# Stage seams of a two-layer decoder step: moved loads, a shorter overflow loop, and unread products on TensorE

## The chip, the cores and the metric

The kernel runs on one core of one Trainium2 chip. The metric is the device time of one execution in microseconds (us), as the median of several runs.

## What is computed

One inference step of a two-layer hybrid decoder: 1,024 prompt tokens and 8 sample tokens of width 1,024, all in 32-bit floats. In each layer an input projection feeds three head groups, a short gated convolution, a latent attention with 8 heads, and an mLSTM with 4 heads. Their outputs are normalised per head and projected back. A hierarchical mixture of 32 experts (two per token) and a gated embedding term follow.

```python
z = jnp.einsum('bld,dn->bln', x, w_in)
q = jnp.einsum('blr,rn->bln', rms_norm(c_q, q_norm_g), w_uq).reshape(B, L, MLA_HEADS, QK_NOPE + QK_ROPE)
h1 = layer_norm(DN_ALPHA * x + jnp.einsum('blm,md->bld', y, w_out), ln1_g, ln1_b)
moe = hier_moe(h1.reshape(B * L, D), w_group, b_group, w_expert, b_expert, e_gate, e_up, e_down).reshape(B, L, D)
ple = jnp.einsum('blp,pd->bld', p, w_pe) * jax.nn.sigmoid(jnp.einsum('bld,de->ble', h1, w_pg))
out = layer_norm(DN_ALPHA * h1 + moe + ple, ln2_g, ln2_b)
```

## The kernel before, in words

The tokens stand in nine tiles of 128 rows: eight of the prompt, and a ninth (`LAST`, also `TP`) with the 8 samples. Each engine has its own program, written out by hand, and the programs meet only in semaphores. A layer has four stages, and each ends in a `Phase`, whose exit is a barrier of all engines, one round for each unbroken range of semaphores that it clears (line 114).

- **Projection** (`stream_project_prepare`). TensorE (PE) walks over the tiles. In step `t` it projects tile `t` in pieces (`part`, lines 507 and 519), and between the pieces it does the small products of tile `u = t - 1`: latents turned (536 to 538), gates turned (545), queries (556), keys (563), values (568), gate columns (573), mLSTM scores (579), queries turned (590). The queue of SyncE (SP) has its own order: in step `t` it stores what tile `u` made, with the store of its turned queries (`QT`) at line 433 and that of the mLSTM output at line 438. In a tenth step (`t == NT`) it loads the first head pair for attention (`first.load_qk`, `first.load_v`, lines 218 to 227), and after that stores the samples' latents (408, 409) and turned queries (433). SP then waits for all its stores (line 449) before it joins the barrier. In layer 1 the stage starts by adding gathered expert rows (DVE line 693, semaphore `added`) to the residual and normalising; PE waits for the result before its first transposes (line 492).
- **Attention** (`attention`) begins with the scores of line 1149, followed by mask, maximum and exponential on DVE and ACT, then transposes (1159).
- **Sample attention** (`sample_attention`) first turns weights (1631 to 1633), waits for copies on DVE, multiplies them with the queries (1636), turns cached pages (1585, 1592), and ends with the product of line 1668.
- **Output, routing and experts** (`mix_route_experts`) begins with products of lines 2259, 2122 and 2148. Later it goes through `EARLY = (0, 1, 2, 3, TP, 4)`: a gate product per tile on PE (2220; 2130 for the samples), its sigmoid on ACT (2474, 2487), a turned embedding input (PE 2187, copied by ACT at 2459, function `p_copied`), and a result stored by ACT to `BASE` (`stored_base`, line 2470, two buffers, semaphore `base_stored`). At the same time the rows are scattered to the experts by GpSimd. Then 21 groups of expert rows run, each stored by ACT at line 2505. Rows over an expert's capacity would go through `rest_turns`, which is in the program of SP, PE, ACT and DVE: two rounds of a loop with sixteen copies of its body each, every copy under an `If`. No line of these bodies shows in the trace.

`combine_last` ends the program: for each tile PE sums the base rows (line 2956) and two gathered expert rows with their weights (2960) in one of four accumulators, then comes a layer norm on DVE and ACT, and a store. SP loads all nine base tiles at once, with gain and bias after the first (2927, 2930), and GpSimd issues all eighteen gathers in a row (2945). PE starts when ACT has made all 18 diagonal weight tiles (`diag_ready`, line 3007).

## Time and profile before

| what | value |
|---|---|
| median of 3 runs | 2455.68 us (2449.44 to 2460.41) |
| the profiled execution, its own time | 2454.07 us |
| its span in the trace | 2452.3 us |
| mean granted TensorE clock | 0.965 |
| busy share of the span: PE, DVE, ACT, POOL | 92%, 47%, 30%, 14% |
| HBM traffic | 208 GB/s over the span |

All rows come from one profiled execution. Times count from the start of its span. A product of 32-bit floats shows as two records on PE, and "x8" counts records. The granted clock is a share of full speed: 1.00 is 2.4 GHz, 0.50 is 1.2 GHz, and a value between them is a stretch with both.

### The profile page before, as it was taken

Reading aid. Unit: us, or ns where it says so; the run is one execution under the profiler, and the core shown is the slowest. Engines: PE = TensorE matmul, PEld = TensorE weight load, DVE = VectorE, ACT = ScalarE, POOL = GpSimd, SP = SyncE. Lnnn points to the kernel's source line nnn. Section 1 sums busy time; section 2 is a strip of 40 time slices with the busy share of each in tenths; the row PEclk is TensorE's granted clock in tenths of the full one; section 3 lists DMA queues with packets and bytes.
Section 4 is the critical chain, followed back from the end, with each engine's and each line's share of the span. In section 5 each row is a group of like instructions: output and inputs, shape, how many; then the busy total and the mean of one; then the engine's idle time right before and its main releaser. Section 6 shows DMA issues by size and latency. Waiting matters only on the chain. (4 is left out here: it accounts for less than half of the span.)

```text
span 2452.3 us, 39565 instructions
## 1 busy us (share of the span) xinstructions
PE 2246.9 (92%) x14448; PEld 1164.2 (47%) x14448; DVE 1160.3 (47%) x2954; ACT 729.4 (30%) x1454; POOL 335.6 (14%) x514
## 2 busy tenths in 40 slices
PE   7999987989999999999599999688889999999977
PEld 3555554557455443333255555455655544333323
DVE  3444444665686312322345554466568752222226
ACT  2555553543211011000145545444323011110012
POOL 1021006830000200000100000296000020000011
PEclk9999998998999999999799999899899999999998
DMA  9476127733510869999753421565323146899976
GB/s 342 161 261 237 59 60 191 198 71 122 193 56 5 347 238 363 406 420 420 260 186 94 129 69 51 151 191 146 122 73 147 31 188 256 343 374 421 420 299 248
DMA packets 229654, 512.00 MB, mean 209 GB/s; under 512 B 60614, under 2 KB 138382, under 8 KB 204088
## 3 DMA queue, kind: packets, MB, share of 16 engines
q1 hardware_dynamic: 182760, 385.68, 43.6%
q0 software_dynamic: 27136, 85.62, 9.8%
q10 hardware_dynamic: 19552, 38.02, 4.2%
q8 instruction: 121, 1.98, 0.3%
q14 instruction: 85, 0.70, 0.1%
HBM read 382.90 MB, written 126.32 MB: 208 GB/s over the span
## 5 line engine op out<-in xcount | busy, mean ns | idle before, releaser
L507 PE MATMUL pj_zp<-pj_w,pj_xT 128*128 128x512 f32 (+1 forms) x1280 | 504.5, 541 | 5.9 <-DMA pj_w<-in_w_in 5.9
L507 PEld LDWEIGHTS pj_zp<-pj_w,pj_xT 128*128 128x128 f32 x1280 | 225.5, 192 | 204.4 <-issue 193.0
L2325 PE MATMUL op_bank<-ex_wgu,h 128*32 128x512 f32 x2688 | 297.1, 594 | 3.2 <-DMA ex_wgu<-in_e_up 3.2
L2148 PE MATMUL op_bank<-op_wout,op_hT 128*128 128x512 f32 x512 | 226.9, 601 | 3.1 <-DVE h L2632 1.7
L2869 DVE TENSOR_TENSOR ex_h<-ex_sil,op_bank 128x256 f32<-128x256 f32 x42 | 17.7, 421 | 367.1 <-ACT ex_sil L2513 367.1
L2325 PEld LDWEIGHTS op_bank<-ex_wgu,h 128*32 128x32 f32 x2688 | 84.5, 110 | 190.6 <-issue 187.4
L2345 PE MATMUL op_bank<-ex_wd,ex_hT 128*32 128x512 f32 x1344 | 154.6, 601 | 8.9 <-DMA ex_wd<-in_e_down 7.4
L2148 PEld LDWEIGHTS op_bank<-op_wout,op_hT 128*128 128x128 f32 x512 | 97.4, 193 | 120.7 <-issue 118.4
L1248 ACT ACTIVATE at_p<-at_s,at_nmx 128x640 f32<-128x640 f32 (+7 forms) x128 | 94.8, 740 | 172.7 <-DVE at_nmx L1211 172.1
L2513 ACT ACTIVATE ex_sil<-op_bank 128x256 f32<-128x256 f32 x42 | 16.1, 383 | 423.7 <-PE op_bank L2325 423.7
L1159 PE MATMUL at_tp<-ident,at_p 128*128 128x128 f32 x576 | 88.3, 281 | 35.8 <-DVE at_pT L1217 25.2
L2220 PE MATMUL op_bank<-op_wpg,op_hT 128*128 128x512 f32 x256 | 115.6, 606 | 0.0
L2111 POOL DMA_INDIRECT scratch_XR<-h,route_row x36 | 36.6, 1018 | 523.8 <-DVEq L2839 513.4
L1209 DVE TENSOR_REDUCE at_mx<-at_s 128x1 f32<-128x640 f32 (+7 forms) x128 | 97.0, 758 | 4.5
L1149 PE MATMUL at_s<-first_qk 96*128 96x512 f32 (+3 forms) x192 | 78.2, 523 | 21.1 <-PEq L114 21.1
L950 ACT ACTIVATE pj_z<-pj_zp 128x512 f32<-128x512 f32 (+1 forms) x80 | 43.2, 540 | 176.3 <-PE pj_zp L507 176.3
L1159 PEld LDWEIGHTS at_tp<-ident,at_p 128*128 128x128 f32 x576 | 62.5, 141 | 65.8 <-issue 60.5
L478 POOL DMA_INDIRECT pj_r<-scratch_YR,route_row x18 | 18.9, 1052 | 540.9 <-issue 357.5
L1207 DVE TENSOR_TENSOR at_s<-at_s,at_mask 128x128 f32<-128x128 f32 x128 | 38.3, 300 | 103.0 <-PE at_s L1149 101.1
L2246 PE MATMUL op_bank<-op_wpg,op_hT 128*128 128x512 f32 x192 | 84.4, 593 | 0.0
L2345 PEld LDWEIGHTS op_bank<-ex_wd,ex_hT 128*32 128x32 f32 x1344 | 40.9, 110 | 91.0 <-issue 84.8
L2220 PEld LDWEIGHTS op_bank<-op_wpg,op_hT 128*128 128x128 f32 x256 | 49.4, 196 | 59.9 <-issue 59.7
(486 smaller groups left out, 3453.2 us busy)
## 6 DMA issues: line engine op xcount, KB each, us to landing
ex_wgu<-in_e_gate SPq DMA_DIRECT2D x64, 1024.0 KB, 11.6
ex_wgu<-in_e_up SPq DMA_DIRECT2D x64, 1024.0 KB, 15.0
ex_wd<-in_e_down SPq DMA_DIRECT2D x64, 1024.0 KB, 18.0
h<-scratch_XR SPq DMA_DIRECT2D x42, 512.0 KB, 16.9
scratch_XR<-pj_zero POOLq DMA_DIRECT2D x38, 512.0 KB, 7.8
pj_w<-in_w_in SPq DMA_DIRECT2D x8, 2048.0 KB, 17.9
pc_ckv<-in_cache_ckv SPq DMA_DIRECT2D x200, 64.0 KB, 2.0
cv_cch<-scratch_Z POOLq DMA_DIRECT2D x48, 256.0 KB, 4.3
```

Of the source, the lines that this page charges most:

```text
L507: last = pe.matmul(zp[c % ZB][:, 0:cn], xT[:, t % 2, k, :], w[:, k, c0:c0 + cn], start=(k == 0), stop=(k == KC - 1), skip_group_check=True)
L950: act.activation(z[:, t % 2, c0:c0 + cn], zp[c % ZB][:, 0:cn], ACT.Copy).then_inc(z_ready, 1)
L1149: last = pe.matmul(scores_of(n)[:, c:min(c + 512, width)], queries(j, s)[:, qb * P:(qb + 1) * P], keys(j, s)[:, c:min(c + 512, width)], st ...
L1159: last = pe.transpose(tp[e][:, kb % 4, :], probs[small(n)][units[n][1]][:, kb, :], ident[:, :])
L1207: st.did(dve.tensor_tensor(diag, diag, mask[:, :], ALU.add))
L1209: st.did(dve.tensor_reduce(mx[:, k:k + 1], out[:, 0:(qb + 1) * P], AX.X, ALU.max))
L1248: act.activation(probs[small(n)][s][:, 0:qb + 1, :].rearrange("p b n -> p (b n)"), scores_of(n)[:, 0:(qb + 1) * P], ACT.Exp, bias=nmx[:, k ...
L2148: last = pe.matmul(op[n][:, :], hT[:, t, c, :], wout[:, c, n * 512:(n + 1) * 512], start=(c == 0), stop=(c == KC - 1))
L2220: last = pe.matmul(gpair[i % 2][n][:, :], hT[:, t, c, :], wpg[:, c, n * 512:(n + 1) * 512], start=(c == 0), stop=(c == KC - 1))
L2246: last = pe.matmul(dbank[:, :], hT[:, DEFERRED[j], c, :], wpg[:, c, n * 512:(n + 1) * 512], start=(c == 0), stop=(c == KC - 1))
L2325: last = pe.matmul(gu[q % 2][part], xT[q % 2][:, c, part], wgu[s][:, :, c, :], start=(c == 0), stop=(c == KC - 1), skip_group_check=True)
L2345: last = pe.matmul(yp[n][part, :], heT[:, q % 2, c, part], wd[s][:, c, n * 512:(n + 1) * 512], start=(c == 0), stop=(c == 1), skip_group_c ...
```

## The change

It has five parts.

1. In the projection stage SP now stores the samples' latents and loads the first head pair inside step `LAST`, ahead of the mLSTM output's store; the tenth step is gone, and the samples' turned queries are stored by ACT at the end of its program (semaphore `q_last`).
2. In the `EARLY` loop, ACT's turn for the samples copies two embedding inputs and issues the base store of the tile before, and only then waits for the older base store and computes the sigmoid.
3. `rest_turns` is one loop over one copy of its body, and the whole loop stands under `If(used > 0)`.
4. In `combine_last`, base loads and gathers run at most two tiles ahead, gain and bias are loaded with tile 2, PE waits for the diagonals of one tile at a time, and the base products run two tiles ahead.
5. `kept_busy` issues products of the identity (128 columns) with the identity repeated four times (512 columns), into a bank that nobody reads. They stand at nine places: four in layer 1 before the first transposes; in both layers 2, 1, 1 and 5 in the projection's tail, 2 after attention, 2 and 3 in sample attention; 2 in `combine_last`.

```diff
@@ -227,6 +227,11 @@
+def kept_busy(pe, bank, ident, count):
+    for _ in range(count):
+        pe.matmul(bank, ident[:, :], ident[:, :].unsqueeze(1).broadcast_to([P, 4, P]), start=True, stop=True)
+
+
 def stream_project_prepare(nc, d, layer, ident, cache, first):
@@ -355,6 +361,24 @@
                     sp.dma_start(w[:, :, c0:c0 + cn], of_layer(d["w_in"], layer).rearrange("(p k) n -> p k n", k=KC)[:, :, c0:c0 + cn]).then_inc(w_loaded[n], 16)
+
+                def latents_stored(u, n):
+                    sp.wait_ge(lat_ready, u + 1)
+                    sp.dma_start(of_layer(d["ckv_all"], layer)[rows(u, n)], ckvn[0:n, :]).then_inc(c_stored, 16)
+                    sp.dma_start(of_layer(d["krope_all"], layer)[rows(u, n)], kpad[0:n, NOPE:]).then_inc(c_stored, 16)
+
+                def first_pair_loaded():
+                    sp.wait_ge(k_stored, 16 * TP)
+                    sp.wait_ge(q_stored, 16 * TP)
+                    sp.wait_ge(normed, NT)
+                    first.load_qk(sp, d, 0)
+                    sp.wait_ge(turned, 2 * NT)
+                    for s in range(2):
+                        sp.wait_ge(y_kept[s], 16 * len(range(s, NT, 2)))
+                    first.load_qk(sp, d, 1)
+                    sp.wait_ge(v_stored, 16 * TP)
+                    sp.wait_ge(o_ready, NT)
+                    first.load_v(sp, d)
@@ -386,27 +410,12 @@
                 sp.wait_ge(cache.table_loaded, 16)
-                for t in range(NT + 1):
+                for t in range(NT):
                     u = t - 1
...
                         load(t + 3)
-                    if t == NT:
-                        sp.wait_ge(k_stored, 16 * TP)
-                        sp.wait_ge(q_stored, 16 * TP)
-                        sp.wait_ge(normed, NT)
-                        first.load_qk(sp, d, 0)
-                        sp.wait_ge(turned, 2 * NT)
-                        for s in range(2):
-                            sp.wait_ge(y_kept[s], 16 * len(range(s, NT, 2)))
-                        first.load_qk(sp, d, 1)
-                        sp.wait_ge(v_stored, 16 * TP)
-                        sp.wait_ge(o_ready, NT)
-                        first.load_v(sp, d)
-                    if is_tile(u):
-                        n = P if u < LAST else DECB
-                        sp.wait_ge(lat_ready, u + 1)
-                        sp.dma_start(of_layer(d["ckv_all"], layer)[rows(u, n)], ckvn[0:n, :]).then_inc(c_stored, 16)
-                        sp.dma_start(of_layer(d["krope_all"], layer)[rows(u, n)], kpad[0:n, NOPE:]).then_inc(c_stored, 16)
+                    if is_chunk(u):
+                        latents_stored(u, P)
                     if t < TP:
@@ -427,12 +436,14 @@
                         sp.dma_start(d["V"][rows(u)], v[:, :]).then_inc(v_stored, 16)
-                    if is_tile(u):
-                        n = P if u < LAST else DECB
+                    if is_chunk(u):
                         sp.wait_ge(qT_out, 2 * u + 2)
-                        sp.dma_start(d["QT"][:, :, rows(u, n)].rearrange("h p n -> p h n"), qT[:, :, 0:n]).then_inc(q_stored, 16)
+                        sp.dma_start(d["QT"][:, :, rows(u)].rearrange("h p n -> p h n"), qT[:, :, :]).then_inc(q_stored, 16)
                     if t + 2 < NT:
                         keep(t + 2)
+                    if t == LAST:
+                        latents_stored(LAST, DECB)
+                        first_pair_loaded()
                     if is_chunk(u):
@@ -442,7 +453,8 @@
                 sp.wait_ge(v_stored, 16 * TP)
-                sp.wait_ge(q_stored, 16 * NT)
+                sp.wait_ge(q_stored, 16 * TP)
+                sp.wait_ge(q_last, 16)
                 sp.wait_ge(y_stored, 16 * TP)
@@ -632,6 +644,9 @@
+                if not entry:
+                    pe.wait_ge(added, 1)
+                    kept_busy(pe, f[0][:, :], ident, 4)
                 rows_turned(0)
@@ -646,6 +661,9 @@
                     part(t, 2)
+                    if t == LAST:
+                        pe.wait_ge(xT_ready, 2 * NT)
+                        kept_busy(pe, f[4][:, :], ident, 2)
                     if is_chunk(u):
@@ -658,6 +676,9 @@
                         values(u)
+                        if t == LAST:
+                            pe.wait_ge(q_out, 2 * u + 2)
+                            kept_busy(pe, f[4][:, :], ident, 1)
                         gate_columns(u)
@@ -668,8 +689,12 @@
                         state_turned()
+                    if t == LAST:
+                        kept_busy(pe, f[4][:, :], ident, 1)
                     if is_tile(u):
                         queries_turned(u)
+                    if u == LAST:
+                        kept_busy(pe, zp[1][:, :], ident, 5)
                     part(t, 8)
@@ -1047,6 +1072,8 @@
                     projected_out(t, 4)
+                act.wait_ge(qT_out, 2 * NT)
+                act.dma_start(d["QT"][:, :, rows(LAST, DECB)].rearrange("h p n -> p h n"), qT[:, :, 0:DECB]).then_inc(q_last, 16)
@@ -1193,6 +1220,7 @@
                         output_turned(n - 2)
+                kept_busy(pe, sc[2][:, :], ident, 2)
@@ -1631,6 +1659,7 @@
                 pe.transpose(misc[0:ROPE, DECB:2 * DECB], krn[:, :], ident[0:DECB, 0:DECB]).then_inc(prep, 1)
+                kept_busy(pe, scp[0][:, :], ident, 2)
                 pe.wait_ge(q_ready, 1)
@@ -1667,6 +1696,7 @@
                 last.then_inc(att_done, 1)
+                kept_busy(pe, scp[0][:, :], ident, 3)
@@ -1855,11 +1884,10 @@
-    with eng.Fori(0, -(-BLOCKS // REST_STEP)) as r:
-        with eng.If(REST_STEP * r < used):
-            for i in range(REST_STEP):
-                with eng.If(REST_STEP * r + i < used):
-                    yield REST_STEP * r + i
+    with eng.If(used > 0):
+        with eng.Fori(0, BLOCKS) as b:
+            with eng.If(b < used):
+                yield b
@@ -2474,17 +2502,20 @@
                 for i, t in enumerate(EARLY):
+                    if t == TP:
+                        p_copied(P_ORDER.index((i, 0)))
+                        p_copied(P_ORDER.index((i - 3, 1)))
+                        stored_base(i - 1)
+                        act.wait_ge(base_stored[i % 2], 16 * (i // 2))
+                        act.wait_ge(g_done, 2 * i + 2)
+                        act.activation(sig[:, i % 2, 0:SCOLS], gpair[i % 2][0][:, 0:SCOLS], ACT.Sigmoid).then_inc(sig_done, 2)
+                        continue
                     if i >= 2:
                         act.wait_ge(base_stored[i % 2], 16 * (i // 2))
-                    if t < TP:
-                        sigmoid(i, 0)
+                    sigmoid(i, 0)
                     if i >= 2:
                         p_copied(P_ORDER.index((i, 0)))
-                    if t < TP:
-                        sigmoid(i, 1)
-                    else:
-                        act.wait_ge(g_done, 2 * i + 2)
-                        act.activation(sig[:, i % 2, 0:SCOLS], gpair[i % 2][0][:, 0:SCOLS], ACT.Sigmoid).then_inc(sig_done, 2)
+                    sigmoid(i, 1)
                     if i >= 3:
@@ -2924,10 +2955,12 @@
                 for t in range(NT):
-                    sp.dma_start(base[:, t, :], d["BASE"][rows(t)]).then_inc(loaded[t], 16)
-                    if t == 0:
+                    if t >= 2:
+                        sp.wait_ge(gathered[t - 2], 32)
+                    if t == 2:
                         for buf, which in ((g, "ln2_g"), (b, "ln2_b")):
                             sp.dma_start(buf[:, :], row_of_layer(d[which], layer)).then_inc(gains, 16)
+                    sp.dma_start(base[:, t, :], d["BASE"][rows(t)]).then_inc(loaded[t], 16)
                 for t in range(NT):
@@ -2939,6 +2972,8 @@
                     m = P if t < TP else DECB
+                    if t >= 2:
+                        pool.wait_ge(gathered[t - 2], 32)
                     if t == TP:
@@ -2947,19 +2982,29 @@
             def _(pe):
-                pe.wait_ge(diag_ready, 2 * NT)
-                for t in range(NT):
+                def bases(t):
                     pe.wait_ge(loaded[t], 16)
...
                         pe.matmul(acc[t % 4][:, n * 512:(n + 1) * 512], ident[:, :], base[:, t, n * 512:(n + 1) * 512], start=True, stop=False)
+
+                def gathered_rows(t):
+                    pe.wait_ge(diag_ready, 2 * t + 2)
                     pe.wait_ge(gathered[t], 32)
...
                         last.then_inc(summed, 1)
+
+                kept_busy(pe, acc[0][:, 0:512], ident, 2)
+                bases(0)
+                bases(1)
+                for t in range(NT):
+                    gathered_rows(t)
+                    if t + 2 < NT:
+                        bases(t + 2)
```

## Rows read from the trace of the kernel before

**Rows 1.** The page's line of the granted TensorE clock, 40 equal slices.
```profile
PEclk9999998998999999999799999899899999999998
```
**Rows 2.** Stages: stretch, length, then busy us (records) of PE, PEld, DVE, ACT, POOL; PEclk, DMA, GB/s.
```profile
340.00:345.00 5.00, 4.97 (x40) 2.29 (x44) 3.65 (x9) 1.53 (x4) 0.00 (x0) 0.68 0.00 1
...
370.00:375.00 5.00, 0.00 (x0) 0.00 (x0) 0.00 (x0) 0.00 (x0) 0.00 (x0) 0.55 1.04 228
...
380.00:385.00 5.00, 5.00 (x14) 2.48 (x13) 2.72 (x7) 1.66 (x4) 3.34 (x9) 0.58 0.95 247
```
**Rows 3.** Timeline of PE, projection's end, layer 0: start, us, instruction, idle before and its releaser.
```profile
339.56 0.38 PE L545 MATMUL pj_f<-ident,ml_gz 128*4 128x128 f32 x2 [1.92 <-DVE ml_gz L769]
...
360.31 0.38 PE L536 MATMUL pj_f<-ident,mp_cqn 128*128 128x128 f32 x2
...
378.69 5.98 PE L1149 MATMUL at_s<-first_qk 96*128 96x512 f32 x10 [10.33 <-PEq L114]
```
**Rows 4.** Timeline of SP's queue over the same stretch.
```profile
358.39 0.32 SPq L433 DMA_DIRECT2D scratch_QT<-mp_qT  x1
...
365.71 0.33 SPq L218 DMA_DIRECT2D first_qk<-scratch_QT  x1
...
367.88 0.39 SPq L227 DMA_DIRECT2D first_v<-scratch_V  x1
```
**Rows 5.** DMA issues from 335 to 382 us: count, KB each, median us to landing.
```profile
first_v<-scratch_V SPq DMA_DIRECT2D x1, 512.0 KB, 8.8
...
scratch_KT<-mp_kT SPq DMA_DIRECT2D x1, 384.0 KB, 3.2
```
**Rows 6.** Timeline, start of sample attention, layer 0.
```profile
556.39 3.58 PE L1636 MATMUL sa_misc<-sa_qT,sa_wukT 64*128 64x8 f32 x16 [1.57 <-DVEq L1720]
...
559.90 3.67 PE L1585 MATMUL sa_tp<-ident,pc_ckv 128*128 128x128 f32 x16
...
564.93 2.02 PE L1585 MATMUL sa_tp<-ident,pc_ckv 128*128 128x128 f32 x16
```
**Rows 7.** Timeline, end of sample attention and start of the output stage, layer 0.
```profile
611.36 1.06 PE L1668 MATMUL sa_misc<-sa_wuv,sa_ol 128*8 128x64 f32 x16 [0.32 <-DVE sa_ol L1755]
...
615.32 0.99 PE L2259 MATMUL op_bank<-ms_g,ms_rep 32*128 32x197 f32 x2 [2.90 <-PEq L114]
...
618.95 9.18 PE L2148 MATMUL op_bank<-op_wout,op_hT 128*128 128x512 f32 x16 [0.73 <-DVE op_hT L2614]
```
**Rows 8.** Timeline, samples' turn of the `EARLY` loop, layer 0.
```profile
828.09 7.03 PE L2220 MATMUL op_bank<-op_wpg,op_hT 128*128 128x512 f32 x16
...
844.93 0.38 ACT L2459 ACTIVATE op_pT<-op_bank 128x256 f32<-128x256 f32 x1 [8.78 <-DMA scratch_BASE<-op_sig]
...
845.46 0.67 PE L2187 MATMUL op_bank<-ident,op_p 128*128 128x128 f32 x2 [2.85 <-ACT op_pT L2459]
...
847.93 9.05 PE L2220 MATMUL op_bank<-op_wpg,op_hT 128*128 128x512 f32 x16
```
**Rows 9.** Timeline of ACT, last issue of layer 0's experts.
```profile
1179.93 0.34 ACTq L2505 DMA_DIRECT2D scratch_YR<-op_hT  x1
```
**Rows 10.** Line 114, the barrier, 1178 to 1187 us: ns min/median/max, first to last start.
```profile
L114 ACTq DRAIN x5: 8/8/8, 1183.5 to 1185.7; - x5
```
**Rows 11.** Timeline of PE, start of layer 1.
```profile
1208.40 14.00 PE L507 MATMUL pj_zp<-pj_w,pj_xT 128*128 128x512 f32 x26 [3.51 <-DMA pj_w<-in_w_in]
```
**Rows 12.** Timeline, `combine_last`.
```profile
2392.04 6.67 PE L2960 MATMUL fi_acc<-fi_r,fi_diag 128*128 128x512 f32 x8 [3.79 <-DMA fi_r<-scratch_YR,route_row]
...
2398.55 1.88 PE L2956 MATMUL fi_acc<-fi_base,ident 128*128 128x512 f32 x4
...
2400.26 3.60 PE L2960 MATMUL fi_acc<-fi_r,fi_diag 128*128 128x512 f32 x8
```
**Rows 13.** The chain of waits: start, us, what.
```profile
2381.51 10.48 DMA fi_r<-scratch_YR,route_row
```
**Rows 14.** DMA issues, 1165 to 1222 us.
```profile
pj_r<-scratch_YR,route_row POOLq DMA_INDIRECT x6, 7.6
```

More of the change, by code:

```diff
@@ L325, in stream_project_prepare @@
             ph.sem(n) for n in ("q_done", "q_out", "k_done", "k_out", "v_done", "v_out", "r_steps", "rope_out", "qt_done", "qT_out"))
-        c_stored, k_stored, v_stored, q_stored, y_stored = (ph.sem(n) for n in ("c_stored", "k_stored", "v_stored", "q_stored", "y_stored"))
+        c_stored, k_stored, v_stored, q_stored, y_stored, q_last = (
+            ph.sem(n) for n in ("c_stored", "k_stored", "v_stored", "q_stored", "y_stored", "q_last"))
         qk_done, qk_out, g_steps, g_neg, g_exp, g_sum, g_ln, gate_ready, gate_done, gate_out = (
@@ L1823 @@
 LEAD = 2
-REST_STEP = 16
 P_ORDER = ((0, 0), (1, 0), (2, 0), (3, 0), (0, 1), (4, 0), (1, 1), (5, 0), (2, 1))
```

## The prediction

> **What bounds the kernel now.** I read the line of the granted clock first [rows 1]: nearly every slice of about 61 us stands at nine tenths of full speed or more, and the dips, eights and sevens, come few and far between. With PE busy for 92% of the span, PE is the bound, and what can be won without less work is its idle time and the time at half clock. The stretches of 5 us show where that is [rows 2]: at the end of the projection PE works at 0.68, then it stands idle while the DMA engines are full (1.04), and it begins attention at 0.58. Rows 3 show the wait itself: 10.33 us ahead of line 1149. SP's queue and the landings [rows 4, 5] say what it waits for: the last load is issued at 367.88 and lands 8.8 us later, at 376.7; the barrier follows. Similar holes stand before sample attention, before the output stage and in the samples' turn [rows 6 to 8], after the experts [rows 9, 10], at the start of layer 1 [rows 11], and ahead of the last sums [rows 12, 13]. Where I saw the stage in layer 0, I count layer 1 as its copy.
>
> **The price of an unread product.** Eight records with 512 columns take 3.60 us at full clock and 6.67 at half [rows 12]; a product is two records, so 0.9 or 1.67 us. The change adds 16 products in layer 0, 20 in layer 1 and 2 at the end: 38, which is 34 us at full and 63 at half clock. They are free only where a wait covers them.
>
> **The change part by part**, as gains:
>
> Projection's tail, the first four products. The two ahead of line 545 fall into its wait of 1.92 us [rows 3]. If they hold the clock, the 4.97 us of busy time at 0.68 [rows 2] shrink by a third, 1.6. I count that once; the two single products and whatever else the tail gains end in front of the loads, which set the stage's end. Bounds 0 and 1.6.
>
> SP's order. The store of the last full tile's turned queries is issued at 358.39 [rows 4], and its twin for the keys lands in 3.2 [rows 5], so it is done at 361.6; the normed latents are ready too, since PE turns them at 360.31 [rows 3]. The loads, now issued at 365.71, can go 4.1 earlier, and so does their end: 376.7 becomes 372.6, attention starts at 374.6, and two layers give **8.2**. Moved behind the loads are the last mLSTM output's store on SP, which finds about 2 MB ahead of it in the DMA engines (some 9 us of loads at 228 GB/s [rows 2]), and the samples' turned queries, which leave by ACT's queue. Both must land before the barrier, which is why I take bounds of 2 and 6 a layer, from half of the gain to half more. SP now waits earlier for the key, query and value stores; queued behind that wait are only those loads and that one store.
>
> Five products in that wait. They take 4.5 us at full and 8.4 at half clock, and the wait that is left is 10.33 − 4.1 = 6.2: they fit if the clock is up. Line 1149 takes 5.98 us at 0.58 [rows 2, 3] and would save about 3. The DMA tail may leave PE idle again after them, so I take 0.8 a layer, **1.6**; bounds 0 and 3 a layer.
>
> Sample attention. The same product group of line 1585 takes 3.67 us early and 2.02 later [rows 6], 1.65 lost to the clock; line 1636 would give half of 3.58, 1.8, and what runs between them about 0.7: up to 4.1 a layer. Two products behind attention may hold back the barrier by 1.8. I take 3 a layer, **6**; bounds −1.8 and 4.1.
>
> Output stage. Line 2148 takes 9.18 us for 16 records where line 2220 takes 7.03 for the same shape [rows 7, 8]: 2.1. Line 2259 gives 0.5 and the products between them about 1.0 by estimate, 3.6 in all. Against that, line 1668 ends at 612.42, and three products last until 615.1, while the stage starts at 615.32 after its barrier [rows 7]. The barrier cannot end before PE joins it, and its rounds are (1185.7 − 1183.5) / 4 = 0.55 us apart [rows 10]; I price the delay at two rounds, 1.1, and take 1.8 a layer after a little more is lost, **3.6**; bounds −2.7 and 3.6.
>
> Samples' turn. ACT stands 8.78 us in front of line 2459, waiting for the base store two tiles back; PE waits 2.85 for that copy and then takes 9.05 for line 2220 in place of 7.03 [rows 8]. With the copies ahead of the wait both go: 2.85 + 2.02 = 4.9, **10** for two layers; bounds 2.85 (the clock stays as it is) and 6. Behind ACT's remaining wait stands only the samples' sigmoid, 8 rows whose result is wanted a tile later.
>
> The overflow loop. ACT issues its last store at 1179.93, done at 1180.27, and the first drain comes at 1183.5 [rows 9, 10]: 3.2 us in which nothing shows but the branches. One test in place of two rounds of tests should leave about 1.2, a gain of 2 a layer, **4**; bounds 0 (a last landing holds the barrier) and 6.4 in all. The Trainium skill (Runtime: NRT & Kernel Launch, Instruction fetch mechanics) says that a branch to a place that isn't fetched yet stalls for a DMA fetch; jumps over large bodies would then be the whole 3.2, and the sum would take 6.4 here. No row above shows such a fetch.
>
> Start of layer 1. PE waits 3.51 us for the weights ahead of line 507 [rows 11], so a faster clock before it gains nothing, and 507 itself can save 14.00 − 26 × 0.45 = 2.3. The four products, 6.7 us at half clock, could overrun that cover by 3.2. I take **0** between −3.2 and 2.3.
>
> `combine_last`. A gather lands after 10.48 us beside the other loads [rows 13], while those at the start of layer 1 take 7.6 [rows 14]: 2.9. The first group of line 2960 loses 6.67 − 3.60 = 3.1 to the clock, and tile 1's base product, some 1.88 with its second half [rows 12], moves ahead into the wait, 1.7: at most 7.7. But base 2 is now loaded only after the first gathers landed, behind gain and bias, and PE comes to it right after the first group; I price that new wait, with the dip that follows it, at 3.7, half of the 7.7. The output store on SP stands behind the base loads and has slack. **4**; bounds 0 and 7.7.
>
> The sum is 1.6 + 8.2 + 1.6 + 6 + 3.6 + 10 + 4 + 0 + 4 = 39. The profiled execution took 2454.07 (its span 2452.3), which gives 2415; the median of the runs is 1.6 higher, so the forecast is **2417**.
>
> **The rivals.** *The products don't hold the clock, only the reorderings count.* For: the waits are cut into pieces by semaphores, and PE at the end of the projection was busy and still at 0.68 [rows 2]. Against: the later groups of a stage show how soon continuous work brings it back [rows 6]. Gain: 8.2 + 2 × 2.85 + 4 = 17.9, time 2438.
> *All of it works.* 1.6 + 8.2 + 6 + 8.2 + 5 + 10 + 6.4 + 6 = 51.4, time 2404; the overflow loop counts here with its full 3.2 a layer. The stall is then in the branches themselves and goes with them. The Trainium skill's section named above states this rule.
> *The samples' turn gives nothing*, because the experts behind it wait for the scatter or for DMA: 39 − 10 = 29, time 2427.
> *Slower: the products stand in the way.* Where a wait is shorter than its products at half clock (1.92 against 3.3 ahead of line 545, 2.90 against 5.0 ahead of the output stage [rows 3, 7]), the engine that waits for PE comes late. If that held for all 38, they would cost 63, the reorderings would give 17.9, and the time would be 2501. It decides from the point at which the products outlast the waits by more than 17.9 + 12 in sum. Against: the waits of 10.33 and of 3.79 [rows 3, 12] are longer than that.
>
> **How the numbers follow.** The forecast gets 0.45, with a range of its own of 2405 to 2429; reorderings alone 0.22; all of it 0.20; no gain in the samples' turn 0.08; slower 0.05. A measurement of this kernel can tell about 0.5%, some 12 us, from no change, so faster means under 2443. The low end, 2402, leaves out the lower half of the case where all works; the high end, 2440, takes in most of the reorderings alone and leaves out the slower case. Faster 0.87, the same 0.08 (the upper end of the reorderings alone), slower 0.05.
>
> **What would show it.** Right: SP's first load of the head pair issued near 361.6 and attention starting near 374.6; a full clock in the first 5 us of attention, sample attention and the output stage; no wait on the base store ahead of line 2459's copy in the samples' turn, and 7.03 for the group after it; a drain about 1 us after ACT's last issue; line 2960's first group at 3.60 and about 3 us earlier. Wrong: PE idle still at the seams with the clock at half behind it; the base store or the mLSTM output's store as the last landing before a barrier; new waits of PE on base tiles in `combine_last`; or unread products as the last instructions of PE ahead of a barrier at which all the others already wait.

## The result and the profile after

The changed kernel takes 2420.0 us (median of 4 runs, 2419.1 to 2420.1), the kernel before 2457.6 beside it: a ratio of 0.9851, with a 95% interval of 0.9832 to 0.9869. The forecast was 2417, the range 2402 to 2440. The profiled execution after has a span of 2418.3 us, 34.0 less than the profiled one before.

On the page, PE's busy share and its clock rose. The chain that ended last has changed hands: before it was mostly PE's last sums,

```profile
PE 2%; DMA 0%; DVE 0%; issue 0%; ACT 0%; POOL 0%; POOLq 0%
```

and now it is DMA and DVE:

```profile
PE 2262.0 (94%) x14524; PEld 1160.5 (48%) x14524; DVE 1159.9 (48%) x2954; ACT 730.4 (30%) x1454; POOL 337.6 (14%) x514
...
PEclk9999999999999999999899999999999999999998
...
DMA 2%; DVE 1%; issue 0%; POOL 0%; ACT 0%; POOLq 0%; SPq 0%; ACTq 0%
```

The dips of [rows 1] are all but gone. PE is busy for 15 us more (2246.9 before; the products), and the program still ends 34 us earlier.

To see where, I cut PE's timeline of each profile at the same instructions: the first product with the input weights, the first of attention, of sample attention, of the output stage, the first and the last of the experts. Lengths in us, layer 0 / layer 1; the columns "again" are second profiles of the same two kernels, and the last two are runs told of below.

| stage | before | before, again | after | after, again | reordering only | products only |
|---|---|---|---|---|---|---|
| projection to attention's start | 361.5 / 361.3 | 359.0 / 362.8 | 355.7 / 359.0 | 355.9 / 358.8 | 358.3 / 359.0 | 357.7 / 359.0 |
| attention | 174.0 / 174.1 | 174.1 / 174.2 | 175.4 / 173.3 | 175.0 / 171.5 | 176.4 / 174.3 | 176.2 / 173.4 |
| sample attention | 62.6 / 63.5 | 62.7 / 63.6 | 59.5 / 60.3 | 59.5 / 60.3 | 62.8 / 62.8 | 59.5 / 60.3 |
| output, routing | 260.1 / 260.3 | 258.3 / 259.9 | 250.5 / 253.4 | 253.4 / 252.3 | 253.9 / 253.6 | 256.0 / 257.9 |
| experts | 303.7 / 305.2 | 307.4 / 305.1 | 304.7 / 304.2 | 304.9 / 305.1 | 305.4 / 304.6 | 304.6 / 305.7 |
| experts' end to layer 1's weights | 29.3 | 29.0 | 26.5 | 26.4 | 26.5 | 29.3 |
| experts' end to the program's end | 79.5 | 78.2 | 78.0 | 78.4 | 77.5 | 87.1 |

The long stages differ by up to 4 us between two profiles of one kernel, so a gain of that size is better read from the instructions at a seam than from a stage's length.

**The projection's seam.** PE's timeline after, against [rows 3]:

```profile
339.55 0.38 PE L557 MATMUL pj_f<-ident,ml_gz 128*4 128x128 f32 x2 [0.21 <-DVE ml_gz L794]
...
359.08 4.54 PE L568 MATMUL pj_f<-mp_wuq,mp_cT 128*128 128x384 f32 x8 [1.01 <-DVE mp_cT L798]
...
366.58 4.46 PE L232 MATMUL pj_zp<-ident 128*128 128x512 f32 x10
373.44 3.26 PE L1176 MATMUL at_s<-first_qk 96*128 96x512 f32 x10 [2.40 <-PEq L114]
```

The wait of 1.92 is 0.21, the five products fit with 2.40 to spare, and the first scores run at full clock (3.26 in place of 5.98). But line 568 takes 4.54 (4.34 in layer 1), where the kernel before had 2.85 in both layers, here layer 0:

```profile
362.39 2.85 PE L556 MATMUL pj_f<-mp_wuq,mp_cT 128*128 128x384 f32 x8 [1.49 <-DVE mp_cT L773]
```

So a dip of the clock stands here that the kernel before did not have: the granted clock over this group is 0.60, before it was 1.00. The queues of SP and of ACT and the landings, against [rows 4, 5]:

```profile
356.87 0.32 SPq L441 DMA_DIRECT2D scratch_QT<-mp_qT  x1
...
360.09 0.32 SPq L218 DMA_DIRECT2D first_qk<-scratch_QT  x1
...
362.18 0.39 SPq L227 DMA_DIRECT2D first_v<-scratch_V  x1
```

```profile
367.51 0.36 ACTq L1076 DMA_DIRECT2D scratch_QT<-mp_qT  x1
```

```profile
first_v<-scratch_V SPq DMA_DIRECT2D x1, 512.0 KB, 8.5
...
scratch_QT<-mp_qT ACTq DMA_DIRECT2D x1, 24.0 KB, 4.4
```

```profile
L114 ACTq DRAIN  x1: 8/8/8, 372.6 to 372.6; - x1
```

The loads leave when the store of the turned queries has landed (356.87 + 3.2 = 360.1), as forecast, and end at 362.18 + 8.5 = 370.7. What lands last is the small store of the samples' queries, now on ACT's queue: 367.51 + 4.4 = 371.9, with the drain at 372.6. 24 KB take 4.4 us behind the loads. It was also what ended the stage before, when SP issued it behind the loads: the last wait of SP ahead of the barrier, before and then after, is for this store.

```profile
SPq L449 <- DMA scratch_QT<-mp_qT: 7.1, 1, 7.1
```

```profile
SPq L458 <- DMA scratch_Y<-ml_y: 6.8, 1, 6.8
SPq L460 <- DMA scratch_QT<-mp_qT: 0.9, 1, 0.9
```

**Sample attention and the output stage**, layer 0, against [rows 6, 7]; the last two lines are layer 1:

```profile
550.00 1.98 PE L232 MATMUL sa_sc<-ident 128*128 128x512 f32 x4
551.91 1.95 PE L1665 MATMUL sa_misc<-sa_qT,sa_wukT 64*128 64x8 f32 x16
553.79 1.97 PE L1613 MATMUL sa_tp<-ident,pc_ckv 128*128 128x128 f32 x16
...
603.88 2.84 PE L232 MATMUL sa_sc<-ident 128*128 128x512 f32 x6
608.36 0.57 PE L2287 MATMUL op_bank<-ms_g,ms_rep 32*128 32x197 f32 x2 [1.64 <-PEq L114]
...
610.76 7.10 PE L2176 MATMUL op_bank<-op_wout,op_hT 128*128 128x512 f32 x16 [0.73 <-DVE op_hT L2645]
...
1782.75 0.99 PE L2287 MATMUL op_bank<-ms_g,ms_rep 32*128 32x197 f32 x2 [2.42 <-PEq L114]
...
1786.38 8.63 PE L2176 MATMUL op_bank<-op_wout,op_hT 128*128 128x512 f32 x16 [0.73 <-DVE op_hT L2645]
```

Sample attention's first groups run at full clock at once (1.97, before 3.67). The output stage starts so in layer 0 (7.10, before 9.18), but not in layer 1 (8.63), though the same three products stand before it. Layer 1 is no copy of layer 0 here: line 114 drains five times in its barrier and three times in layer 0's, and PE idles 2.42 us behind the products in place of 1.64.

**The samples' turn**, against [rows 8]: the wait of 2.85 and the dip behind it are gone. From the samples' gate products to the end of the large group the turn takes 12.0 us in both layers, where it took 17.9 / 17.3 before and 16.3 / 18.2 in the second profile of the kernel before.

```profile
831.89 0.50 PE L2215 MATMUL op_bank<-ident,op_p 128*128 128x128 f32 x2
832.33 1.07 PE L2158 MATMUL op_bank<-op_wpe,op_pT 128*32 128x256 f32 x16
833.33 7.13 PE L2248 MATMUL op_bank<-op_wpg,op_hT 128*128 128x512 f32 x16
```

**The experts' end**, against [rows 9, 10]: ACT's last store is done at 1164.72, and the first drain, with which the barrier begins, follows after 0.9 us in place of 3.2. In layer 1 it is 0.9 in place of 2.0.

```profile
1164.38 0.34 ACTq L2536 DMA_DIRECT2D scratch_YR<-op_hT  x1
```

```profile
L114 ACTq DRAIN  x5: 8/8/8, 1165.6 to 1167.6; - x5
```

**Layer 1's start**, against [rows 11]: PE still waits for the weights after its four products.

```profile
1177.12 6.05 PE L232 MATMUL pj_f<-ident 128*128 128x512 f32 x8 [13.53 <-DVE first_qk L718]
1184.62 1.16 PE L504 MATMUL pj_f<-ident,first_qk 128*128 128x128 f32 x8 [1.44 <-DVE first_qk L741]
1190.14 5.49 PE L519 MATMUL pj_zp<-pj_w,pj_xT 128*128 128x512 f32 x6 [4.37 <-DMA pj_w<-in_w_in]
```

**The last sums**, against [rows 12, 13]: timelines of PE, SP and ACT, then from the chain of waits (start, us, what) the landings of two gathers and of the first output store.

```profile
2353.57 3.67 PE L2997 MATMUL fi_acc<-fi_r,fi_diag 128*128 128x512 f32 x8 [1.05 <-DMA fi_r<-scratch_YR,route_row]
2362.79 3.72 PE L2990 MATMUL fi_acc<-fi_base,ident 128*128 128x512 f32 x4 [5.54 <-DMA fi_base<-scratch_BASE]
```

```profile
2386.98 26.94 SPq L2966 DMA_DIRECT2D out_y_all<-fi_o  x9
```

```profile
2392.92 1.20 ACT L3060 ACTIVATE fi_o<-fi_acc,fi_shift,fi_rs 128x1024 f32<-128x1024 f32 x1 [6.13 <-DMA out_y_all<-fi_o]
```

```profile
2346.94 6.50 DMA fi_r<-scratch_YR,route_row
...
2355.54 10.07 DMA fi_r<-scratch_YR,route_row
...
2386.98 5.85 DMA out_y_all<-fi_o
```

The first gathers land in 6.50 in place of 10.48, and their group runs at full clock and early, as forecast. Then PE waits 5.54 for base tile 2 and multiplies it at half clock (3.72 for 1.88). A later gather takes 10.07 again, and each tile's pair of gathers now waits for that of two tiles before. SP issues the first output store only at 2386.98, behind base loads that wait for gathers, and ACT stands 6.13 us for it. From SP's first base load to the end the stage takes 2418.3 - 2344.74 = 73.6 us; before it was 2452.3 - 2379.32 = 73.0.

### The profile page after: what moved, and what is told of

It reads as the page before. It is cut to its first block and busy times, and to the rows that moved or that the text cites. A ratio compares the mean times of both kernels' runs of the same rounds, so it can differ in the third digit from the quotient of the medians.

```text
span 2418.3 us, 39662 instructions
## 1 busy us (share of the span) xinstructions
PE 2262.0 (94%) x14524; PEld 1160.5 (48%) x14524; DVE 1159.9 (48%) x2954; ACT 730.4 (30%) x1454; POOL 337.6 (14%) x514
## 5 line engine op out<-in xcount | busy, mean ns | idle before, releaser
L2900 DVE TENSOR_TENSOR ex_h<-ex_sil,op_bank 128x256 f32<-128x256 f32 x42 | 17.7, 422 | 366.6 <-ACT ex_sil L2544 366.6
L2544 ACT ACTIVATE ex_sil<-op_bank 128x256 f32<-128x256 f32 x42 | 16.1, 384 | 423.5 <-PE op_bank L2353 423.5
## 6 DMA issues: line engine op xcount, KB each, us to landing
ex_wgu<-in_e_gate SPq DMA_DIRECT2D x64, 1024.0 KB, 11.1
pj_w<-in_w_in SPq DMA_DIRECT2D x8, 2048.0 KB, 17.9
cv_cch<-scratch_Z POOLq DMA_DIRECT2D x48, 256.0 KB, 4.2
```

## Experiments

The theory: reorderings and products gain separately, seam by seam, as the prediction's terms say. The rivals: only the reorderings count; the products are in the way; the gain of the last stage is real, or isn't.

**Reordering only.** All nine calls of `kept_busy` and their three waits are taken out.

```diff
-                kept_busy(pe, sc[2][:, :], ident, 2)
...
-                kept_busy(pe, scp[0][:, :], ident, 3)
```

> The changed kernel without any of its unread products; all reorderings stay. If the products hold the clock (forecast), their gains go stage by stage: in each layer about 4.1 us at the start of sample attention, 1.8 at the start of the output stage, some 2 at the start of attention, and 1.5 once in the projection's tail, in sum about 17 us: a median near 2437, with half clock again at those starts. If only the reorderings count (rival), the median stays at 2420 within 4 us. If the products stand in the way, it falls below 2416.

Measured: 2430.5 (ratio 0.9894, 0.9877 to 0.9911), where 2437 was expected. The products are worth 10.5 us by the medians and 13.6 by the spans (2431.9 and 2418.3): neither nothing nor 17. By the table above, 3.3 and 2.5 of it are sample attention and 2.6 layer 0's seam; layer 1's seam is as long without the products as with them. The samples' turn takes 12.0 us in both layers here too, so its gain needs no products.

**Products only.** The same nine calls put into the kernel before.

```diff
+                kept_busy(pe, sc[2][:, :], ident, 2)
...
+                kept_busy(pe, scp[0][:, :], ident, 3)
```

> The kernel before with all 38 unread products put in, and no reordering. If products and reorderings add up, it takes 2457.6 - 17 = 2440 us, give or take 4, with the samples' turn waiting 2.9 us on PE and the first drain of an experts' end some 3 us after ACT's last issue as before. If the products alone bring nothing (rival), 2457; if they need the reorderings to be covered (slower side), over 2460.

Measured: 2438.9 (0.9931, 0.9914 to 0.9948), as expected. Against before, reordering alone gains 26.1 and products alone 17.7; both together gain some 37, not 44. The table shows one place of the overlap: either alone shortens layer 1's seam by 2.4, both by 2.3. Where the other 5 us of overlap lie stays open. The profiled execution, at 2445.97, is this kernel's longest, and its last stage tells why: after ACT's last store of layer 1 was issued no engine worked for 10 us, while the instruction queues moved eight packets (view of the DMA queues and of line 114).

```profile
2357.96 0.34 ACTq L2526 DMA_DIRECT2D scratch_YR<-op_hT  x1
```

```profile
q8 instruction: 4, 0.07, 2.6%
q14 instruction: 4, 0.03, 0.8%
```

```profile
L114 POOLq DRAIN  x5: 34/34/41, 2368.4 to 2371.3; - x5
```

**The last sums as before.** The function `combine_last` is that of the kernel before, so without its two products.

```diff
-                    if t >= 2:
-                        sp.wait_ge(gathered[t - 2], 32)
...
-                kept_busy(pe, acc[0][:, 0:512], ident, 2)
...
+                pe.wait_ge(diag_ready, 2 * NT)
```

> The changed kernel with the last stage (combine_last) of the kernel before. The traces give 73.0 us from the last barrier to the end before, and 73.6 after. If that stage gains nothing by the change (theory from the traces), the median is 2419 within 2 us, with the last stage at about 73.0. If the forecast's 4 us are in it and something else in the layers lost them (rival), it is 2424.

Measured: 2423.2 (2422.9 to 2423.6). The total speaks for the rival, the stages don't: the experts of layer 1 end at 2345.3 in its profile, against 2340.3 after, in code that is the same up to there. From there on the old last stage takes 76.6 us, the new one 78.0 and, in its second profile, 78.4. So the new form lost 1.4 to 1.8 there, and a difference of 3 us between medians of such kernels can come from elsewhere.

**Three tiles ahead, stores in between.**

```diff
-                    if t >= 2:
-                        sp.wait_ge(gathered[t - 2], 32)
-                    if t == 2:
-                        for buf, which in ((g, "ln2_g"), (b, "ln2_b")):
-                            sp.dma_start(buf[:, :], row_of_layer(d[which], layer)).then_inc(gains, 16)
+                    if t >= 3:
+                        sp.wait_ge(gathered[t - 3], 32)
                     sp.dma_start(base[:, t, :], d["BASE"][rows(t)]).then_inc(loaded[t], 16)
+                    if t == 3:
+                        for buf, which in ((g, "ln2_g"), (b, "ln2_b")):
+                            sp.dma_start(buf[:, :], row_of_layer(d[which], layer)).then_inc(gains, 16)
+                    if t >= 6:
+                        row_stored(t - 6)
...
-                    if t >= 2:
-                        pool.wait_ge(gathered[t - 2], 32)
+                    if t >= 3:
+                        pool.wait_ge(gathered[t - 3], 32)
```

> The changed kernel, with loads and gathers of the last stage three tiles ahead in place of two, gain and bias after the fourth base tile, and SP's output stores between its loads. If the stage now waits for its own window and for SP's order (theory: 5.5 us of PE on base tile 2, its half clock, and 6.1 us of ACT on the first output store), PE runs from its first gathered tile without a break: about 9 us less, 2411, last stage near 64. If the DMA engines are the bound there (rival), gathers land after 10 us again and the gain is 2 us at most: 2418 or more.

Measured: 2417.2 (0.9834, 0.9815 to 0.9852), 6.0 below the run with the old last stage, measured beside it. PE and SP of that stage:

```profile
2368.97 3.60 PE L3002 MATMUL fi_acc<-fi_r,fi_diag 128*128 128x512 f32 x8
2373.49 1.98 PE L2995 MATMUL fi_acc<-fi_base,ident 128*128 128x512 f32 x4 [0.93 <-DMA fi_base<-scratch_BASE]
```

```profile
2373.29 0.34 SPq L2959 DMA_DIRECT2D out_y_all<-fi_o  x1
```

The wait of 5.54 is 0.93, ACT's is gone, and from SP's first load (2349.44) to the end (2416.2) the stage takes 66.8: 6.8 of the 9 expected. Window and queue order were the new bound of this stage. But the rival holds in part: gathers land in 9.2 in the median, 7.3 in the changed kernel, and in the chain that ended last stands a base load of 12.41:

```profile
2361.03 12.41 DMA fi_base<-scratch_BASE
```

The whole program gained less than its stage: 2417.2 is 2.8 below 2420.0, where 9 was expected. Two edits went together here; their shares were not tried apart.

**Sixteen copies behind one test.**

```diff
     with eng.If(used > 0):
-        with eng.Fori(0, BLOCKS) as b:
-            with eng.If(b < used):
-                yield b
+        with eng.Fori(0, -(-BLOCKS // step)) as r:
+            with eng.If(step * r < used):
+                for i in range(step):
+                    with eng.If(step * r + i < used):
+                        yield step * r + i
```

> The changed kernel, with the two rounds of sixteen copies of the overflow body put back, all under the one test used > 0. One jump passes over the whole code. If the time at the experts' end is a stall for instructions at the jump's far target (theory: the instruction queues move 4 to 8 packets there before, 0 or 1 after), the first drain comes 2 us or more after ACT's last issue again, with packets on those queues, and the median is 2 to 5 us above the changed kernel. If it is the number of tests run (rival), the drain comes after about 1 us as in the changed kernel and the time is the same.

**One copy, no test around the loop.**

```diff
-    with eng.If(used > 0):
-        with eng.Fori(0, BLOCKS) as b:
-            with eng.If(b < used):
-                yield b
+    with eng.Fori(0, BLOCKS) as b:
+        with eng.If(b < used):
+            yield b
```

> The changed kernel with its one copy of the overflow body in the loop, but without the test around the loop: each of the loop's rounds tests and jumps over a short body. If the stall is for instructions at a far target, the instruction queues stay quiet and only the tests themselves are left: some 17 rounds of 0.1 to 0.3 us by estimate, 2 to 5 us a layer. If jumps alone cost nothing (rival), the drain comes after 1 us and the time is that of the changed kernel.

Measured: 2426.4 (2421.1 to 2432.9) and 2460.8 (2454.9 to 2465.4), against 2420.7 for the changed kernel measured beside them. With the copies behind one test, ACT's last store of layer 0 is done at 1168.28, and:

```profile
L114 ACTq DRAIN  x5: 8/8/8, 1170.5 to 1172.6; - x5
```

```profile
q8 instruction: 2, 0.03, 1.5%
q14 instruction: 3, 0.02, 0.9%
```

With one jump over the long code the drain comes after 2.2 us, in layer 1 after 1.9, in place of 0.9, and the instruction packets are back: the jump costs 1.3 and 1.0 us. In layer 1 the barrier behind it is longer as well, 2.8 us from its first drain to its last in place of 2.0 (3.0 in the kernel before). This makes some 3 of the 5.7 us between the medians. With one copy and all tests ACT is done at 1168.12, no instruction packet moves in that stretch, and the drain comes 20.4 us later:

```profile
L114 ACTq DRAIN  x5: 8/8/8, 1188.5 to 1190.6; - x5
```

So both halves of the edit count. The short body spares the jump's price, and the one test spares 17 rounds of the loop, which take (20.4 - 0.9) / 17 = 1.15 us each, far above the 0.1 to 0.3 expected. The Trainium skill (Runtime: NRT & Kernel Launch, Instruction fetch mechanics) states that a taken branch to code that isn't in the fetched pages waits for a DMA fetch; the packets beside the 2.2 us agree. How the 3.2 and 2.0 us of the kernel before divide is not shown: at 1.15 us a round its two rounds alone would make 2.3, the whole gain of layer 0 and twice that of layer 1 (1.1).

**The changed kernel again**, unaltered.

> The changed kernel, unaltered, beside the others of this call. Expected within 4 us of 2420; its attention stages and its starts of the output stage show how much of a stage's time wanders from run to run without any edit (theory: 1 to 2 us in attention, about 1.2 at the start of the output stage, by where the clock dips).

Measured: 2420.7 (2419.6 to 2424.7). Stages without an edit moved by up to 3 us (attention of layer 1 by 1.8, the output stage of layer 0 by 2.8), above the 1 to 2 expected.

**Without the four products of layer 1's start**, on top of the three tiles.

```diff
-                if not entry:
-                    pe.wait_ge(added, 1)
-                    kept_busy(pe, f[0][:, :], ident, 4)
```

> The kernel with the last stage three tiles ahead, and without the four unread products at the start of layer 1. PE waits for the input weights there in any case (4.4 us after). If those products bring nothing (forecast: 0), the time is that of the three-tiles kernel within 2 us, about 2415 to 2419, and line 519 of layer 1 starts about 26.4 us after the experts' end. If they hold the clock for the first tiles of layer 1 (rival), it loses 2.3 us there.

Measured: 2416.7 (0.9843, 0.9826 to 0.9860). From the experts' end to the weights' first product it takes 26.4 us with and without: they bring nothing. This version is 4.0 below the changed kernel measured beside it, whose ratio there is 0.9862 (0.9842 to 0.9883); the intervals overlap.

**Without the five ahead of attention; without the three behind sample attention.**

```diff
-                    if u == LAST:
-                        kept_busy(pe, zp[1][:, :], ident, 5)
```

```diff
-                kept_busy(pe, scp[0][:, :], ident, 3)
```

> The changed kernel without the five unread products in the wait ahead of attention. If they are what brings attention to full clock (forecast), its first ten records of scores take about 6 us again in place of 3.3, in both layers. If attention then comes out longer by 2 to 3 us as a whole, the gain is kept; if it stays within 1 us of the 175.4 and 173.3 us of the changed kernel (rival), the early gain is given back to dips later in the stage.

> The changed kernel without the three unread products behind sample attention. The barrier then comes about 1.5 us earlier in each layer (sample attention's second part 41.9 in place of 43.4 us in layer 0). If the products hold the clock (forecast), the first group of the output projection takes 9.2 us again in place of 7.1 where they had held it (layer 0 of the changed kernel), net loss about 1.8 us. If the clock falls there with or without them (rival; it did in layer 1 of the changed kernel), leaving them out gains 1.5 us a layer.

Measured, one run each: 2419.5 and 2424.7. Without the five, attention starts at half clock in both layers and takes 176.1 and 174.7 us, within 1.1 of the changed kernel's two profiles in layer 0, and 1.4 to 3.2 longer in layer 1. Both lie within what the nine profiles with the five span (173.7 to 176.2 and 171.5 to 175.6), so no gain in attention as a whole is shown. Without the three, sample attention's second part (from the fourth group on) is 1.5 us shorter and the output stage longer. From sample attention's fourth group of turned pages to the experts it takes 296.1 / 296.8 us; with the three it is 294.0 / 297.6 and 296.8 / 296.5. On average the three gain 0.2 a layer, which these runs can't tell from nothing.

**The kernel before again.**

> The kernel before, unaltered, for a second profile of it. If attention's length belongs to the kernel, it is 174.0 and 174.1 us again within 0.3. If it wanders from run to run with the places where the clock dips (theory from the two profiles of the changed kernel, 171.5 to 175.4), it differs by 1 us or more, and no gain or loss below 2 us in attention can be put down to an edit.

Measured: 2453.6, attention 174.1 / 174.2 us. My theory falls for this kernel: in two profiles its attention does not wander. It starts at half clock each time; in the changed kernel it starts now at full clock, now at half. Other stages of the kernel before do wander: layer 0's projection by 2.5, its experts by 3.7. The granted clock in the first 5 us of a stage, layer 0 / layer 1:

| kernel | attention | sample attention | output projection |
|---|---|---|---|
| before, twice | 0.50 / 0.50, 0.50 / 0.50 | 0.50 / 0.50, 0.50 / 0.50 | 0.58 / 0.65, 0.58 / 0.64 |
| reordering only | 0.50 / 0.50 | 0.50 / 0.67 | 0.57 / 0.64 |
| after | 1.00 / 0.66 | 1.00 / 1.00 | 1.00 / 0.69 |
| after, again | 0.50 / 1.00 | 1.00 / 1.00 | 0.59 / 0.66 |
| without the five | 0.50 / 0.50 | 1.00 / 1.00 | 1.00 / 0.66 |
| without the three | 0.66 / 0.50 | 1.00 / 1.00 | 0.52 / 0.55 |

In the nine profiles so far with the five products, attention starts at 1.00 in 2 of 18 cases and at 0.66 to 0.68 in eight more; without them it starts at 0.50 every time. In the ten with those around sample attention, that stage starts at 1.00 in 20 of 20. In the nine with the three behind it, the output projection does so in layer 0 in 7 of 9, in layer 1 in none, with PE idle behind them for 1.6 to 1.7 us in layer 0 and 2.4 in layer 1.

**Few products.** The version without four, also without the five and the three; eight are left in the tails (the expectation says ten, a miscount), eight around sample attention, two in the last stage.

> The three-tiles kernel without the four products at the start of layer 1, the five ahead of attention and the three behind sample attention; ten of its 38 stay in the projection's tails and eight around sample attention, two at the end. If the gain of the products sits at sample attention and in the tails (theory from the clocks of the runs so far: 1.00 in every start of sample attention, but at attention's start in 2 of 18 and at layer 1's output stage in none of 9), the median is that of the kernel without four, 2416.7, within 3 us. If the five and the three carry their forecast (2 x 0.8 and 2 x 1.8 us, rival), it is 2421 to 2423.

Measured: 2418.4 (2414.4 to 2420.8; 0.9843, 0.9823 to 0.9863), 1.7 above the version without four, within the 3 us: the 20 products left out carry no gain that these runs can show.

## Why the prediction was right, step by step

The likeliest case came, and the gain was 37 to 38 us by the medians where 39 was forecast. That it came so close is partly luck: four terms fell short by 11.5 us together, three came out 5.2 above their price, and the medians lie 3.6 further apart than the two profiled executions. Forecast against these two profiles, both layers together:

| step | forecast | measured | from |
|---|---|---|---|
| tail and SP's order | 9.8 | 8.2 | stage 361.5 / 361.3 to 355.7 / 359.0 |
| five products, attention | 1.6 | -0.6 | attention 174.0 / 174.1 to 175.4 / 173.3 |
| start of sample attention | 6 | 9.3 | its start to the fourth group of turned pages, 20.7 / 20.8 to 16.1 / 16.1 |
| three products, output's start | 3.6 | 0.5 | -1.5 twice; 3.3 and 0.2 gained |
| samples' turn | 10 | 11.1 | 17.9 / 17.3 to 12.0 / 12.0 |
| overflow loop | 4 | 4.8 | 29.3 to 26.5; 6.5 to 4.4 before the last stage |
| four products, layer 1 | 0 | 0 | the run without them |
| last sums | 4 | -0.6 | 73.0 to 73.6 |

What is left to the 34.0 between the spans is 1.9 in the rest of the output stage, -0.6 at the program's start and 0.1 in the experts, all within what a stage moves without an edit.

- **SP's order** gave its 4.1 in both layers: the first load leaves 3.2 us after the store of the last full tile's turned queries in place of 7.3, in both profiles of either kernel. **The tail's clock** gave its 1.6 once, as counted. From the first small product of the tail to that store it takes 19.9 us in every run with the products; without them it takes 19.9 or 21.4, in the kernel before 21.4 / 19.9 in one profile and 19.9 / 21.5 in the other, with the reordering only 21.3 / 21.4. So the dip can stand in either layer or in both. What the sum had wrong is what ends the stage. It read the last load there, and it is the samples' query store, which waits for PE to turn those queries and does not follow the loads. Counted from the stage's first product with the weights, it leaves 2.8 us earlier in layer 0 and 0.1 later in layer 1, and lands in 4.4 and 4.7 us, where SP had waited 7.1 and 6.8 for it. From the first load to the drain it takes 12.5 and 12.7 us, before 12.1 and 11.8, which loses 1.3 us; the rest of the 1.6 that are missing lies in the first tiles, which wander by up to 2 us. By the second profiles the stage gained 7.1 in place of 8.2.
- **Attention's start** was priced at a quarter of its possible gain (0.8 of 3 a layer); a full clock came in 2 of 18 cases, and attention as a whole is no shorter.
- **Sample attention** was mis-sized downwards, 3 a layer for 4.6. I had cut the gain of up to 4.1 for the products behind attention, which might hold back the barrier by 1.8, and those cost 0.5 (from attention's last own product to the next stage 2.66 us, before 2.20).
- **The output's start.** In layer 0 the delay (1.5 for 1.1 forecast) and the gain gave 1.8, as forecast; in layer 1 the clock fell all the same. The step that failed is counting layer 1 as a copy of layer 0: its barrier has two rounds more, and PE idles 0.8 us longer behind the products. That this alone lets the clock fall was not tried.
- **The samples' turn** gained 5.9 and 5.3, for 4.9 forecast, and 4.3 and 6.2 against the second profile of the kernel before. The sum of the dip took the large group only, and left out the two short ones between the wait and that group (0.50 and 1.07 after; 0.67 and 1.94 before).
- **The overflow loop**: size right, and of the mechanism one half. That a jump over long code costs time was only offered as one rule; the run with sixteen copies behind one test shows it, at 1.3 and 1.0 us. The tests, taken for cheap, cost 1.15 us a round in a loop of 17; how much of the kernel before was rounds and how much jumps stays open.
- **The last sums** fell outright. The step was the price of the new wait and its dip, "half of the 7.7" with no row behind it (5.54 and 1.84 measured, 7.4 for 3.7), and "the output store on SP stands behind the base loads and has slack". It had none: the store left at 2386.98, when tile 6 had been gathered, and ACT had stood for it since 2386.8. The shorter landing of the first gathers, 2.9 forecast, came (4.0), and the new waits took it back.

Of the rivals, *reorderings alone* was 2438. The kernel without the products measured 2430.5, and the changed kernel 2420.0, so the products do count; that rival's price, 17.9, was also some 8 too small, 5 of it the samples' turn (11.1 for 2 x 2.85). The reorderings were not taken out one by one, apart from the loop and the last sums; the shares of the others are read from their rows. *The products in the way* is refuted as a whole (products only: 17.7 faster), but it is what happens behind sample attention, where they cost 1.5 us a layer and pay it back only in layer 0, in most runs.

## What to carry to other kernels

Work that only keeps the clock up paid here where it ended close to the real work that followed it, as in sample attention; ahead of a longer barrier or a load it brought a gain in some runs and none in others, so look at more than one profile before counting it. When loads in a queue are held back to make the first ones quicker, go through everything queued behind them: here that was the output store, and one tile more of window with the stores in between was worth 6.8 us of that stage and 3 to 4 of the whole. A loop that nearly never runs wants both a test around all of it and a short body.

## What the runs showed that was not expected

One round of a loop whose body is skipped costs 1.15 us here (17 rounds, 20.4 us against 0.9). With sixteen copies of a body to jump over, the drain behind the experts came 1.9 to 3.5 us after ACT's last issue in seven cases and 10 us after it in one, with four to eight instruction packets each time; with one copy behind one test it came after 0.9 at most. A store of 24 KB from 96 partitions took 4.4 us to land beside 2 MB of loads, half as long as the 512 KB load (8.5). And the same program, run twice, held the clock at attention's start in layer 0 once and in layer 1 once (1.00 / 0.66, 0.50 / 1.00); what decides that stays open.
